# A hybrid trunk on one core: the low part of every fourth weight slab of the convolution stage, formed by accumulating DMAs instead of a VectorE subtraction

## The reference, cut to what matters

```python
def _even_mixer(h, w_in, a_conv, b_conv, b_conv_bias, b_ln_g, b_ln_b, w_out):
    p = h @ w_in                                  # (512 x 2048) @ (2048 x 7168)
    a_x, a_b, a_c, a_z, b_val, b_gate, b_z = jnp.split(p, 7, axis=-1)
    ya = a_b * _causal_dwconv(a_c * a_x, a_conv)  # 3 taps
    yb = b_val * jax.nn.sigmoid(b_gate)
    yb = _causal_dwconv(yb, b_conv) + b_conv_bias # 31 taps
    yb = jax.nn.silu(_layernorm(yb, b_ln_g, b_ln_b))
    u = jnp.concatenate([ya * jax.nn.silu(a_z), yb * jax.nn.silu(b_z)], axis=-1)
    return u @ w_out
```

## Time and profile before

| | us |
|---|---|
| time, two runs | 1404.67 and 1405.18, median 1404.93 |
| span of the profiled execution | 1402.8 |
| PE busy | 1377.8 (98%) |
| DVE busy | 698.9 (50%) |
| ACT busy | 384.5 (27%) |
| POOL busy | 109.9 (8%) |

### The profile page before, as it was taken

The page is one execution under the profiler, slowest core; times in us unless marked ns, Lnnn a source line. Parts: engine busy times, 40 slices in busy tenths (PEclk is TensorE's granted clock), DMA queues, the critical chain, the costliest instruction groups (busy, mean ns, idle before and its releaser), DMA issues.

```text
span 1402.8 us, 16146 instructions
## 1 busy us (share of the span) xinstructions
PE 1377.8 (98%) x6466; PEld 1156.4 (82%) x6466; DVE 698.9 (50%) x767; ACT 384.5 (27%) x413; POOL 109.9 (8%) x101
## 2 busy tenths in 40 slices
PE   5999999999999999999999999999999999999997
PEld 4988888888888888888888899888888888888886
DVE  7588888888753223334332585444522222722333
ACT  5332233222222122223321353222222223512220
POOL 5100000000008200000000000000000003400000
PEclk9999999999999999999999999999999999999999
DMA  8243333434243333333422364333333322262204
GB/s 245 61 111 95 94 112 98 120 90 112 71 127 90 109 90 91 90 105 137 178 90 95 119 205 121 92 99 105 96 90 100 109 90 90 64 236 90 90 30 180
DMA packets 208307, 154.82 MB, mean 110 GB/s; under 512 B 2576, under 2 KB 187024, under 8 KB 205968
## 3 DMA queue, kind: packets, MB, share of 16 engines
q1 hardware_dynamic: 207120, 145.94, 35.1%
q10 hardware_dynamic: 1152, 8.39, 1.6%
HBM read 145.93 MB, written 8.39 MB: 110 GB/s over the span
## 4 chain that ended last, share of the span: by engine, by line
PE 96%; DVE 2%; issue 1%; DMA 0%; ACT 0%; DVEq 0%; POOLq 0%; POOL 0%
PE bank L417 32%; PE bank L418 32%; PE bank L419 32%; DVE h_lo L971 1%; DVE scratch L977 1%; PE bank L447 0%; DVE rows L964 0%; DMA rows<-x_t 0%; DVE diagonals L942 0%; DVE w_lo L986 0%; DVE rows L1128 0%; PE bank L476 0%; PE bank L485 0%; ACT scratch L682 0%; PE bank L545 0%
## 5 line engine op out<-in xcount | busy, mean ns | idle before, releaser
L417 PE MATMUL bank<-h_hi,w_hi 128*128 128x512 f32 (+1 forms) x1600 | 597.3, 373 | 4.9 <-DVE h_lo L971 4.8
L418 PE MATMUL bank<-h_lo,w_hi 128*128 128x512 f32 (+1 forms) x1600 | 595.3, 372 | 0.0
L419 PE MATMUL bank<-h_hi,w_lo 128*128 128x512 f32 (+1 forms) x1600 | 595.3, 372 | 0.0
L909 DVE TENSOR_TENSOR w_lo<-raw,w_hi 128x2048 fp32r<-128x2048 f32 x121 | 280.3, 2317 | 215.7 <-ACT w_hi L650 194.7
L417 PEld LDWEIGHTS bank<-h_hi,w_hi 128*128 128x128 f32 x1600 | 301.4, 188 | 59.3 <-issue 4.5
L419 PEld LDWEIGHTS bank<-h_hi,w_lo 128*128 128x128 f32 x1600 | 301.4, 188 | 52.6
L418 PEld LDWEIGHTS bank<-h_lo,w_hi 128*128 128x128 f32 x1600 | 301.4, 188 | 52.4 <-issue 0.5
L650 ACT ACTIVATE w_hi<-raw 128x2048 fp32r<-128x2048 f32 x122 | 233.3, 1912 | 238.2 <-PE bank L419 189.6
L1004 DVE SCALAR_TENSOR_TENSOR rows<-shifted,vecs,rows 128x512 f32 x256 | 198.0, 776 | 42.2 <-ACT rows L720 10.9
L417 PE MATMUL bank<-w_hi,h_hi 128*128 128x512 f32 x512 | 199.5, 390 | 0.0
L419 PE MATMUL bank<-w_hi,h_lo 128*128 128x512 f32 x512 | 199.3, 389 | 0.0
(11 more groups left out here) (79 smaller groups left out, 442.6 us busy)
## 6 DMA issues: line engine op xcount, KB each, us to landing
raw<-e_in SPq DMA_DIRECT2D x54, 1024.0 KB, 5.6
raw<-o_in SPq DMA_DIRECT2D x32, 1024.0 KB, 6.0
raw<-e_out SPq DMA_DIRECT2D x16, 1024.0 KB, 5.1
raw<-o_out SPq DMA_DIRECT2D x16, 1024.0 KB, 5.0
rows<-x_t SPq DMA_DIRECT2D x8, 512.0 KB, 6.5
x_mid<-rows ACTq DMA_DIRECT2D x4, 1024.0 KB, 4.8
raw<-o_cw SPq DMA_DIRECT2D x4, 1024.0 KB, 5.3
out<-rows SPq DMA_DIRECT2D x3, 1024.0 KB, 3.9
```

What stands on the lines that cost most here:

```text
L417: nc.tensor.matmul(dst, w[0], m[0], start=first, stop=False)
L418: nc.tensor.matmul(dst, w[0], m[1], start=False, stop=False)
L419: return nc.tensor.matmul(dst, w[1], m[0], start=False, stop=last)
L909: nc.vector.tensor_tensor(w_lo[:, slot, :], raw[:, slot % RAW, :], f32(w_hi[:, slot, :]), ALU.subtract)\
```

## The change

For slab 4c+4 of each step (slot 0: the next step's gate slab, and after the last step the slab of `A_B`) the low part is no longer subtracted on DVE. ACT writes the negated high part into `w_lo` (`minus_hi`, the same input and the same rounding, scale -1), right behind its high part. POOL waits for it and issues eight DMAs that add the weights themselves from HBM to what stands in `w_lo`: each covers 128 partitions x 2 rows of 128 float32, so 256 pieces of 512 bytes, 128 KB; the eight raise the semaphore `lo_added` by 128 in all. DVE, which had formed this low part ahead of its gated product, now waits for `lo_added` after its first ten taps and adds the one to `lo_ready` itself. The other three slabs of a step are split as before.

```diff
+        minus_hi_ready = sem("minus_hi_ready")
+        lo_added = sem("lo_added")
@@ gpsimd
+            e_in_rows = e_in.rearrange("(k p) n -> p k n", p=P)
             for c in range(CB):
+                pool.wait_ge(minus_hi_ready, c + 1)
+                first = B_GATE + (c + 1) * P if c + 1 < CB else A_B
+                for j in range(8):
+                    nc.gpsimd.dma_start(
+                        w_lo[:, 0, j * HALF:(j + 1) * HALF].rearrange("p (k c) -> p k c", c=P),
+                        e_in_rows[:, j * 2:(j + 1) * 2, first:first + P],
+                        accum_op=ALU.add).then_inc(lo_added, 16)
                 pool.wait_ge(conv_done, c + 1)
                 nc.gpsimd.tensor_tensor(csum, csum, tile(c + CB), ALU.add)\
                     .then_inc(csum_ready, 1)
@@ scalar
+            def minus_hi(slot):
+                nc.scalar.activation(w_lo[:, slot, :], raw[:, slot % RAW, :], ACT.Copy,
+                                     scale=-1.0).then_inc(minus_hi_ready, 1)
@@ scalar, step c
                 nc.scalar.activation(sig, bank[0][:, :], ACT.Sigmoid).then_inc(bank_free[0], 1)
                 split_ahead(c, 1)
+                minus_hi(0)
                 act.wait_ge(bank_free[1], c + 2)
@@ vector, step c
             with dve.Fori(0, E1A) as c:
                 chain[1] = c * links
-                split_ahead(c, 1)
                 dve.wait_ge(slab_done, done(c * SLOTS + 2))
@@
                 convolve(c, conv_done, glu, CONV_B, "conv_b", 1, 11)
+                dve.wait_ge(lo_added, c * 128 + 128)
+                dve.sem_inc(lo_ready, 1)
                 split_ahead(c, 2)
```

## The result

| | before | after |
|---|---|---|
| time, two runs each | 1404.67 to 1405.18, median 1404.93 us | 1532.41 to 1532.74, median 1532.58 us |
| ratio | | 1.0909, 95% interval 1.0885 to 1.0932 |
| span of the profiled execution | 1402.8 us | 1530.3 us |
| PE busy | 1377.8 us | 1395.9 us |

What follows compares the result with a forecast made beforehand. The prediction took PE, busy 98% of the span, to bound the kernel. First stall 20.1, seven later 9.4 each and clock 1.5 made 87.4 us, so 1404.9 became 1492 us, 6.2% slower; range 1409 to 1560.

Steps and rivals of the forecast that it cites:

- Bound by PE, DVE's relief worth nothing: Convolution stage: PE never waits there, so removing 18.3 us of DVE's subtractions can't shorten it.
- The first step: Slab 4's release moves behind DVE's ten taps: PE stalls 4.0 us even with free DMAs, 20.1 us with T = 26.1.
- T: Time a step's eight DMAs take, the unknown: bounds 5.6 and 48 us, taken as 26.1 us.
- The loop over POOL's sum: Later steps: next release 26.85 + T after this one, needed every 43.5; each of seven is T - 16.7 late, 9.4 us.
- One after another: The eight DMAs land in turn, 3.26 us each, because POOL's descriptor reserve is small; T = 26.1 us, chance 0.60.
- the prediction's own sign of being wrong: Wrong if eight DMAs land within 16 us of the first's issue, or a single one takes much more than 3.3 us.
- The formula: Time lost: (T - 6.0) for the first stall, plus 7(T - 16.7) for later releases, plus 1.5 us for the clock.
- The clock: PE at half clock after each stall; only what follows the last stall is on the path, 1.5 us, between 0 and 3.
- The hidden case: Rival: the DMAs overlap, T = 12, only a first stall of 6.0 us; 1412 us, chance 0.27.
- The dearer case: Rival: describing costs POOL two 0.54 us instructions more per DMA, 4.34 us each, T = 34.7; 1561 us, chance 0.12.
- The loop over ACT: Rival: the loop closes over ACT's negated copy, not POOL's sum; free T 20.5, 1466 us, chance inside the 0.60.
- The page's figure for a DMA: Skill's fit for a POOL-issued DMA: 2.3 us for 128 KB, eight in turn 18.4 us, total 26 us and not 87.

Runs made afterwards that it cites:

- The last kernel: All three together on the changed kernel: reserve 2048 bytes, channel sum behind the next step's DMAs, step 0's low part on DVE; 1413.4 us, ratio 1.0061.
- sixteen DMAs: Changed kernel, reserve 1024, same adds of 512-byte rows cut into sixteen DMAs of 128 pieces (64 KB) instead of eight of 256; 1518.4 us, ratio 1.081.
- sum behind: Changed kernel with POOL's channel sum of a step queued behind the next step's DMAs and not ahead of them; 1506.2 us, ratio 1.072.
- reserve 1088: Changed kernel with the reserve for descriptors of POOL's DMAs at 1088 bytes and not 1024; 1479.1 us, ratio 1.053.
- six of eight: Changed kernel with six of the eight DMAs, so two eighths of this low part stay the negated high part; 1470.4 us, ratio 1.047.
- reserve 2048: Changed kernel with the reserve for descriptors of POOL's DMAs at 2048 bytes a partition and not 1024; 1449.3 us, ratio 1.031.
- rows of 1 KB: Changed kernel, reserve 1024, each adding DMA reading one 1024-byte row per partition, 128 pieces and not 256; 1431.3 us, ratio 1.019.
- the run without DMAs: Changed kernel with the DMAs left out; DVE waits for ACT's negated copy and releases the slab behind its ten taps; 1411.5 us, ratio 1.0045.
- The plain copies: Changed kernel with the eight DMAs as plain copies instead of adds, same 256 pieces each, reserve 1024; 1414.6 us, ratio 1.007.
- reserve 2112: Changed kernel with the reserve for descriptors of POOL's DMAs at 2112 bytes and not 1024; 1449.5 us, ratio 1.032.
- the kernel with the first step by DVE: Changed kernel, but step 0 forms its low part on DVE as before and the DMAs begin with step 1; 1508.7 us, ratio 1.074.

## Why the prediction was right or wrong, point by point

**Bound by PE, DVE's relief worth nothing.** Right. The last kernel shows it best: with nearly all waits gone, it stands 8.6 us over the kernel before (1413.41 against 1404.81) and not under it.

**The first step.** Right. The taps alone put the release 3.8 us too late (4.0 predicted). With the DMAs the stall was 24.4 us and not T - 6.0 = 20.1, which is the size of T again.

**The loop over POOL's sum.** Right in place: 26.85 us from release to POOL's start were predicted, 27.15 measured (101.11 to 128.26), and moving the sum took it out. It shows that the order in one engine's queue was worth 26 us. The round was forecast at 53 us and measured 57.8; all but 0.3 us of the difference is T.

**The size of T.** The term that was mis-sized. One after another was right, and the prediction called it a choice, not a row; the runs with another reserve show that the reason it gave, the small room, was the right one. But a DMA took 3.8 us, not 3.26, which comes near the prediction's own sign of being wrong ("much more than 3.3 us"). The two terms of the sum were close: the DMA engines move one for about 1.1 us (0.96 taken), and it lands after 3.5 us (3.26 taken). The rest is POOL, which starts the next one 0.3 us after that. Over eight, T was 30.3 and not 26.1, and the 4.2 us count eight times, 34 us. That is most of the 40 us between 1492 and 1532.6; the loop's missing 0.3 us makes 2 more, the clock 1, and T grew to 30.7 in the later steps (57.8 - 27.15), which is another 2 to 3.

**The formula.** The runs allow a test of how lateness adds up: lateness of the first release against 76.4, plus seven times what the round exceeds 43.5, plus 2.3 us of half clock. Lateness and round are read from each trace, so the table tests the adding up and not the size of T.

| kernel | first release, late by | round | sum | measured over before |
|---|---|---|---|---|
| changed | 24.7 | 57.8 | 127.2 | 127.7 |
| sixteen DMAs | 25.2 | 55.8 | 113.6 | 113.5 |
| sum behind | 25.2 | 54.0 | 101.1 | 101.2 |
| reserve 1088 | 17.3 | 51.3 | 74.3 | 74.2 |
| six of eight | 16.7 | 50.1 | 65.2 | 65.5 |
| reserve 2048 | 15.3 | 47.4 | 45.1 | 44.3 |
| rows of 1 KB | 12.4 | 45.3 | 27.0 | 26.3 |

**The clock.** Its place was right: the eight stalls cost PE 18.1 us of busy time, 2.3 each on average, but only the last one's part is on the path, since the loop hides the others. The sum in the table closes with one 2.3. I had taken 1.5. What the granted clock did (busy by stretch; the columns are PE, PEld, DVE, ACT, POOL, clock, DMA share, GB/s):

```profile
76.50:77.00 0.50, 0.26 (x3) 0.05 (x1) 0.35 (x2) 0.00 (x0) 0.00 (x0) 1.00 0.52 65
...
80.00:81.00 1.00, 0.00 (x0) 0.00 (x0) 0.31 (x1) 0.00 (x0) 0.00 (x0) 1.00 0.44 52
81.00:82.00 1.00, 0.00 (x0) 0.00 (x0) 0.00 (x0) 0.00 (x0) 0.00 (x0) 0.56 0.65 79
...
101.00:102.00 1.00, 0.84 (x2) 0.76 (x3) 0.89 (x1) 0.00 (x0) 0.00 (x0) 0.50 0.00 0
...
104.00:105.00 1.00, 1.00 (x4) 0.81 (x3) 0.82 (x2) 0.00 (x0) 0.00 (x0) 0.50 1.16 327
105.00:106.00 1.00, 1.00 (x5) 0.82 (x5) 0.75 (x1) 0.00 (x0) 0.00 (x0) 0.99 1.27 305
```

PE stops at 76.8, the clock goes to 1.2 GHz after 81, PE resumes at 101.2 and has 2.4 GHz again at 105. In the run without DMAs, whose one stall is 3.8 us (PE stands from 76.5 to 80.2), the granted clock is halved from 79.5 on and full again near 86.

**The rivals.** The hidden case (1412, T = 12, one stall of 6.0 us) wasn't met by the adds. The plain copies are that case, with T = 12.9, one stall of 7.0 us and 1414.6 us, so its price was right. That the last kernel, at 1413.4, stands near it too is a coincidence: there the first stall was taken away and a later one of 4.3 us came up. The dearer case (1561) took 1.08 us of POOL's time per DMA, close to the 1.2 measured, but placed it beside the landing: one DMA would be 4.34 us. Measured were 3.8, since POOL's time lies inside the 3.5 us from issue to landing. The loop over ACT came true once the sum was moved.

**The page's figure for a DMA.** By the Trainium skill, *DMA: Bandwidth & Descriptors*, section "Anatomy of one DMA", eight in turn would have been an estimated 18.4 us. Measured were 30.3. Part of the gap is the adding: a plain copy of 128 KB landed in 2.7 us here (2.3 by the page), an add in 3.5. The measurement decides.

## What to carry to other kernels

Before work is moved from an engine to DMAs that POOL issues, ask how many of them can be in flight: the reserve for their descriptors may hold one, and then the price is landing time times their number (eight of 128 KB took 30.3 us here, where moving one kept the DMA engines busy for about 1.1 us); an adding DMA took twice the room of a copy, and 64 bytes more of reserve were worth 53 us. Follow the whole loop from release to release, through each queue that an instruction stands in; under the threshold it costs nothing, above it each microsecond counts once per step. And if the engine that sets the end never waits for the one you relieve, the best case is no change.

## What the runs showed of the hardware that I had not expected

- **POOL waits by the DMA's number, not by what is in flight.** With room for three adding DMAs (reserve 2048), POOL issued 3, 3, 1, 1 in the first step, and 1, 3, 2, 1, 1 in the next. Number the DMAs of a kernel from 1 on through all steps, and the singles have an order: POOL waits behind each third and behind each seventh. It is as fixed in the other kernels. "Entries" is the reserve over 16 bytes; the third column is what one DMA takes of them, counted as above (256 pieces are 16 for each DMA engine, 128 are 8; an added one takes two reads, and one entry is added on each side):

| kernel | entries | reads, writes | POOL waits behind each |
|---|---|---|---|
| changed | 64 | 33, 17 | DMA |
| reserve 1088 | 68 | 33, 17 | second and third |
| reserve 2048, all three together | 128 | 33, 17 | third and seventh |
| reserve 2112 | 132 | 33, 17 | third and seventh |
| rows of 1 KB, sixteen DMAs | 64 | 17, 9 | third and seventh |
| plain copies | 64 | 17, 17 | third |

The last column gives all 198 waits inside the steps of the seven kernels where more than one fits, and no other. It is what two reserves of this many entries would do, one for reads and one for writes, if entries don't run over the end, the last entry is never filled (4 x 33 = 132 holds three, 4 x 17 = 68 holds three), and POOL waits for all that is in flight before it begins one of the two anew. So the idea behind the run with 2112 bytes may hold, and its forecast failed on the full last entry and on the writes. This was read out of the traces afterwards; no run was made to test it.
- **POOL's work on a DMA goes by pieces and by adding**: 1.21 us for 256 added pieces, 0.88 us for 128, 0.72 us for 256 copied ones. The packet count doesn't show the second read: 17408 packets for 64 DMAs are 272 each, 256 pieces and 16 more, with adds and with copies alike.
- **DVE didn't slow POOL.** Issued while DVE ran its taps (74.72, 78.54) a DMA took POOL 1.24 and 1.21 us, issued while DVE stood still (86.09) 1.20. The Trainium skill, *SBUF — State Buffer*, section "Who interferes with whom", says that a DVE instruction with two inputs in SBUF gets in the way of POOL's reads of SBUF and not of its writes, and infers that making descriptors needs the writes. The trace agrees.
- **Taps with fixed addresses are faster.** Where the first step is written out ahead of the loop, ten taps take 7.84 us; in the loop, where the address of the tap comes from a register, 8.82 us. DVE's timeline in the kernel with the first step by DVE:

```profile
72.52 7.84 DVE L1026 SCALAR_TENSOR_TENSOR rows<-shifted,vecs,rows 128x512 f32<-128x512 f32 x10 [0.95 <-ACT rows L738]
...
138.76 8.81 DVE L1026 SCALAR_TENSOR_TENSOR rows<-shifted,vecs,rows 128x512 f32 x10
```

That the register is the cause is argued and not shown: in the loop the count that each tap waits for comes from a register too. The difference itself is 1 us for ten taps, about 3 us over a step of 32, and that is also the lead of POOL's first DMA in that run.
